# Windows of the projections in another column order, with heads, Fourier products and turns between them

## The reference

```python
for l in range(2):                                  # first_block
    mod = silu_c @ w_ada[l] + b_ada[l]              # 1024 -> 6*1024: shifts, scales and gates
    mc = silu_cc @ w_ada[l][:, :n_c] + ...          # the same for the context tokens
    hx = rmsnorm(x) * (1 + sc_a) + sh_a             # hc likewise from ctx
    ux = hx @ w_in[l]                               # 1024 -> 2304 columns
    uc = hc @ (w_in[l] if l == 0 else w_in[l][:, OFF_K:OFF_HQ])
    fx = fourier_mix(ux[0:256], w_four[l])          # FFT over tokens and channels, then a product
    ax = attention(rope(rmsnorm(q)), rope(rmsnorm(k)), v)   # 8 query heads, 2 key heads of 64
    rx = hgrn_scan(...)                             # gated recurrence in chunks
    x = x + g_a * (concat(fx, ax, rx) @ w_out[l])
    x = x + g_f * swiglu(rmsnorm(x) * (1 + sc_f) + sh_f, w_gate[l], w_up[l], w_down[l])
    # the context likewise in layer 0
for i in range(2):                                  # second_block
    mod = silu(c_2) @ ada_w[i] + ada_b[i]
    h = rmsnorm(x) * (1 + sc1) + sh1
    x = x + g1 * banded_or_dilated_attention(h @ w_in) @ w_out   # 1536 or 2304 columns
    x = x + g2 * swiglu(...)
return rmsnorm(x) * final_norm
```

## Time and profile before

| | us |
|---|---|
| three runs, median (lowest to highest) | 2167.18 (2163.68 to 2167.72) |
| profiled execution | 2165.82 |
| its span in the trace | 2163.9 |
| its mean granted clock of TensorE | 0.896 |

### The profile page before, as it was taken

How to read it: one execution, slowest core, us unless ns; L and a number is a source line. 1 busy time by engine, 2 the same in 40 slices (tenths; PEclk the granted TensorE clock), 3 DMA queues, 4 the chain that set the end, 5 groups by cost and what they waited for, 6 DMA issues and landing times.

```text
span 2163.9 us, 30885 instructions
## 1 busy us (share of the span) xinstructions
PE 1828.9 (85%) x12238; PEld 1639.6 (76%) x12238; DVE 1353.1 (63%) x2508; ACT 834.7 (39%) x1600; POOL 59.9 (3%) x133
## 2 busy tenths in 40 slices
PE   4697688889999998894778699967789989588997
PEld 2696576788887887792567699866689979478996
DVE  1667868456776556527775578856658874565544
ACT  3422453233221321522642344345534435454442
POOL 0000012000000000000020000000000000000000
PEclk8899778789999999896778799987899999699999
DMA  8544010026555553333212688642279865004653
GB/s 283 177 152 136 1 59 21 1 79 175 157 184 156 165 161 129 118 105 98 78 40 78 182 253 273 228 130 54 78 228 273 268 223 152 24 18 121 188 172 136
DMA packets 358990, 300.60 MB, mean 139 GB/s; under 512 B 7920, under 2 KB 333280, under 8 KB 358464
## 3 DMA queue, kind: packets, MB, share of 16 engines
q1 hardware_dynamic: 357456, 294.22, 44.7%
q0 software_dynamic: 1392, 4.42, 0.9%
HBM read 297.56 MB, written 1.05 MB: 138 GB/s over the span
## 4 chain that ended last, share of the span: by engine, by line
PE 72%; DVE 14%; ACT 5%; issue 5%; DMA 4%; SPq 0%; DVEq 0%; ACTq 0%; POOLq 0%
PE bank L793 69%; PE bank L807 3%; ACT whigh L1271 1%; DMA A<-in_w_ada 1%; DVE ACC L1688 1%; ACT PB L1424 1%; DVE A L1769 1%; DMA raw<-in_ffn_w_in 1%; DVE A L1953 1%; DVE HTL L1775 1%; DMA raw<-in_w_up 0%; DMA X<-in_ctx 0%; DVE nw L1707 0%; DVE rs L1709 0%; DVE nw L1708 0%
## 5 line engine op out<-in xcount | busy, mean ns | idle before, releaser
L1672 DVE TENSOR_TENSOR wlow<-raw,whigh 128x2048 fp32r<-128x2048 f32 (+1 forms) x183 | 410.0, 2244 | 328.7 <-ACT whigh L1271 328.0
L1271 ACT ACTIVATE whigh<-raw 128x2048 fp32r<-128x2048 f32 (+1 forms) x183 | 343.2, 1878 | 585.1 <-PE bank L793 362.4
L793 PE MATMUL bank<-HTH,whigh 128*128 128x256 f32 (+1 forms) x1424 | 447.7, 314 | 12.5 <-DVE HTL L1775 12.5
L793 PE MATMUL bank<-HTL,whigh 128*128 128x256 f32 (+1 forms) x1424 | 443.1, 311 | 0.0
L793 PE MATMUL bank<-HTH,wlow 128*128 128x256 f32 (+1 forms) x1424 | 442.8, 311 | 0.0
L793 PE MATMUL bank<-whigh,HTH 128*128 128x256 f32 (+1 forms) x1008 | 292.2, 290 | 12.7 <-DVE HTL L1775 6.0
L793 PEld LDWEIGHTS bank<-HTH,whigh 128*128 128x128 f32 x1424 | 277.1, 195 | 26.0 <-issue 13.6
L1688 DVE SCALAR_TENSOR_TENSOR ACC<-A,cond,ACC 128x256 f32<-128x256 f32 x602 | 282.9, 485 | 17.5
L793 PE MATMUL bank<-wlow,HTH 128*128 128x256 f32 (+1 forms) x1008 | 290.3, 288 | 0.0
L793 PE MATMUL bank<-whigh,HTL 128*128 128x256 f32 (+1 forms) x1008 | 290.0, 288 | 0.0
L793 PEld LDWEIGHTS bank<-HTH,wlow 128*128 128x128 f32 x1424 | 276.5, 194 | 13.2
(11 more groups left out here) (214 smaller groups left out, 2278.9 us busy)
## 6 DMA issues: line engine op xcount, KB each, us to landing
...
```

The source lines that it names most:

```text
L793: return nc.tensor.matmul(out, lhsT, rhs, start=start, stop=stop, skip_group_check=True)
L1271: nc.scalar.activation(parts(loads[n])[0], raw_slot(loads[n]), ACT.Copy).then_inc(*made("split_high", loads[n]))
L1672: V.tensor_tensor(low, raw_slot(loads[n]), as_float(high), ALU.subtract).then_inc(*made("split_low", loads[n]))
```

## The change

It does these things:

- `win_order` gives the windows another order: 0, 3, 1, 2, 4 to 8 in layers 0 and 1 (window 3 holds keys and values), keys and values first in layers 2 (4, 5, 0 to 3) and 3 (6, 7, 8, 0 to 5). `load_plan` and `proj_jobs` follow it.
- In layers 0 and 1 the Fourier products stand after the second tile of the second window, the gains with it, and DVE makes tile t's heads in the window at position t + 3; PE turns the tile after the second tile of the window at position t + 5 (`turns_after`). In layers 2 and 3 the keys are turned one window after the keys' last one, and the queries one window behind their own.
- The heads are now computed in place in `U` and not through a buffer of `A`; `values_low` is a function of its own.
- The chunk sums: two chunks in each of the first four windows of layer 0 instead of one in each of eight; the four chunks in layer 0's heads and the four in layer 1's heads (computed by PE) go; 35 instead of 27 stand beside the feed forward of layer 0. The slots of the first eight lie now in `U`'s columns 1280 to 2304 (`AWU`), two instead of three, and each load is two DMAs of 512 KB.
- The first chunk loads of a feed forward wait for PE's product `h` of the last tile (at the feed forward's start) instead of `g`. `gate_rows` of layer 0's feed forward is moved from `gu` 0 to `gu` 9.
- The load of `w_four` on POOL waits for the turned keys of the layer's last tile.
- Buffers change places to make room: the conditioning bias goes to `U`'s tile 2, the query halves and turned probabilities of layer 3 are swapped in `A`, copies of the keys for the dilated groups are made tile by tile.

The diff, cut to its core:

```diff
+def win_order(layer):
+
+    return ((0, 3, 1, 2, 4, 5, 6, 7, 8), (0, 3, 1, 2, 4, 5, 6, 7, 8), (4, 5, 0, 1, 2, 3), (6, 7, 8, 0, 1, 2, 3, 4, 5))[layer]
...
-    return [(j, t) for j, (a, b) in enumerate(col_groups(layer)) for t in tiles_of(layer, "mix") if cols_of(layer, t, a, b)]
+    groups = col_groups(layer)
+    return [(j, t) for j in win_order(layer) for t in tiles_of(layer, "mix") if cols_of(layer, t, *groups[j])]
...
+def turns_after(layer, j, n):
+
+
+    at = win_order(layer).index(j)
+    if layer < 2:
+        return [("tile", at - 5)] if n == 1 and at >= 5 else []
+    last_k = win_order(layer).index((DH * (HEADS_Q[layer] + HEADS_K[layer]) - 1) // 256)
+    first_q = win_order(layer).index(0)
+    out = [("keys", n)] if at == last_k + 1 else []
+    if n == 1 and at > first_q:
+        out.append(("queries", j - 1))
+    return out
...
+GATES_AT = 9
...
-    give([("win", 0, j) for j in range(8)] + [(0, "heads", t) for t in range(4)] + scan(0, 4))
-    give(feed_forward(0, 27))
-    give([(1, "heads", t) for t in range(4)] + scan(1, 6))
+    give([("win", 0, j) for j in win_order(0)[0:4] for _ in range(2)] + scan(0, 4))
+    give(feed_forward(0, 35))
+    give(scan(1, 6))
...
+        AWU = [U[:, t:t + 2, 1280:2304].rearrange("p t (k c) -> p t k c", k=4) for t in (2, 0)]
...
-            slots = {"start": (0, 1, 2, 3), "projection": (2, 3, 4), "feed_forward": (2, 3, 4)}.get(group[0], (0, 1))
+            slots = {"start": (0, 1, 2, 3), "projection": (5, 6), "feed_forward": (2, 3, 4)}.get(group[0], (0, 1))
...
-                    sp.wait_ge(*upto("product", "mod", 0, STARTING - 1))
+                    sp.wait_ge(*(upto("product", "bias") if slot == 5 else upto("sums_set")))
                 elif group[0] == "feed_forward":
 
-                    sp.wait_ge(*upto("product", "g", group[1], "ffn", 1 if group[1] == 0 else 0, 1))
+                    sp.wait_ge(*upto("product", "h", group[1], "ffn", tiles_of(group[1], "ffn")[-1], 1))
                 w, b = ada_w(l)
-                sp.dma_start(dst, w.rearrange("(p k) c -> p k c", k=8)[:, :, 256 * j:256 * j + 256]) \
-                    .then_inc(*made(f"ada_weights{slot}", l, j, by=16))
+                src = w.rearrange("(p k) c -> p k c", k=8)[:, :, 256 * j:256 * j + 256]
+                if slot < 5:
+                    sp.dma_start(dst, src).then_inc(*made(f"ada_weights{slot}", l, j, by=16))
+                else:
+                    for half in range(2):
+                        sp.dma_start(dst[:, half], src[:, 4 * half:4 * half + 4]).then_inc(*made(f"ada_weights{slot}", l, j, by=16))
...
-                    pool.dma_start(W4, io["w_four"][l].rearrange("(k p) c -> p k c", p=P)).then_inc(*made("gains_in", l, by=16))
...
+                    pool.wait_ge(*upto("product", "kT", l, tiles_of(l, "mix")[-1], 0))
+                    pool.dma_start(W4, io["w_four"][l].rearrange("(k p) c -> p k c", p=P)).then_inc(*made("four_in", l, by=16))
...
             def project(l):
-                for j, (a, b) in enumerate(col_groups(l)):
+                for at, j in enumerate(win_order(l)):
                     key = ("win", l, j)
                     need_parts(key)
                     wh, wl = (w.rearrange("p (k c) -> p k c", k=KD) for w in parts(key))
-                    for t in [t for j2, t in proj_jobs(l) if j2 == j]:
-                        if j == 0 or (l == 1 and t >= 2):
+                    for n, t in enumerate([t for j2, t in proj_jobs(l) if j2 == j]):
+                        if at == 0 or (l == 1 and t >= 2):
                             h_ready(l, "mix", t)
                         ps = open_bank("u", l, j, t)
                         r = slice(P * t, P * t + P)
                         for k in range(KD):
                             last = mm3(ps[:, 0:256], (HTH[:, k, r], HTL[:, k, r]), (wh[:, k, :], wl[:, k, :]), k == 0, k == KD - 1)
                         last.then_inc(*made("product", "u", l, j, t))
+                        if l < 2 and at == 1 and n == 1:
+                            for g in range(2 if l == 0 else 1):
+                                fourier(l, g)
+                        for turns in turns_after(l, j, n):
+                            head_turns(l, *turns)
                     late(key)
                 late(None)
+                modulation_end()
+                if l >= 2:
+                    head_turns(l, "queries", DH * HEADS_Q[l] // 256 - 1)
...
+                        if (l, f) == (0, GATES_AT):
+                            gate_rows(l, "ffn")
...
             def project(l):
-                for j in range(len(col_groups(l))):
+                for at, j in enumerate(win_order(l)):
                     split(index[("win", l, j)] + HIGH)
-                    beside("win", l, j)
+                    if l < 2:
+                        if at == 1:
+                            for g in range(2 if l == 0 else 1):
+                                fourier(l, g)
+                        if at == 2:
+                            gains(l)
+                        beside("win", l, j)
+                        if 5 <= at < 8:
+                            heads_low(l, "tile", at - 5)
+                        if 3 <= at < 7:
+                            heads(l, at - 3)
+                    else:
+                        for turns in turns_after(l, j, 0) + turns_after(l, j, 1):
+                            heads_low(l, *turns)
+                        if j == (DH * (HEADS_Q[l] + HEADS_K[l]) - 1) // 256:
+                            for t in X_TILES:
+                                heads(l, t)
+                    if j == value_group(l):
+                        values_low(l)
+                if l < 2:
+                    heads_low(l, "tile", 3)
+                else:
+                    heads_low(l, "queries", DH * HEADS_Q[l] // 256 - 1)
...
-                need_u(l, tiles[-1], PROJ[l] - 256, PROJ[l]) if l != 1 else need_u(l, tiles[-1], OFF_I, OFF_HQ)
-                need_u(l, 1, PROJ[l] - 256, PROJ[l])
-                for n, t in enumerate(tiles):
-                    if n:
-                        lows(tiles[n - 1])
...
+                if t:
+                    dve.wait_ge(*upto("product", "kT", l, t - 1, 0))
...
@@ -2173,11 +2262,6 @@
                 if l:
                     split(index[last_down(l - 1)] + HIGH)
                 project(l)
-                if l < 2:
-                    gains(l)
-                    for g in range(2 if l == 0 else 1):
-                        fourier(l, g)
-                heads(l)
                 attention(l)
                 if l < 2:
                     recurrence(l)```

What this does to the engines' lists at the places where the time is set. SyncE at the start of layer 0's projection, before (L629 loads projection weights, L592 a chunk's weights; each waits for the product or the sum that frees its buffer):

```order
L629 DMA raw<-in_w_in 128x8x256 [waits product]
L592 DMA A_53<-in_w_ada 128x8x256 [waits product] x3
L592 DMA A_53<-in_w_ada 128x8x256 [waits ada_sum]
L629 DMA raw<-in_w_in 128x8x256 [waits product]
L592 DMA A_53<-in_w_ada 128x8x256 [waits ada_sum]
L629 DMA raw<-in_w_in 128x8x256 [waits product]
```

269 lines of the change are left out of this document (146 added, 123 removed).

## The result

The changed kernel takes 2111.8 us (median of four runs, 2109.38 to 2114.55) against 2167.45 us (2163.68 to 2168.07): a ratio of 0.9747, with a 95% interval of 0.973 to 0.9764. The profiled execution took 2112.47 us, its span is 2110.2. The forecast was 2101, its range 2086 to 2124. So 55.6 us were won where 66.4 were forecast.

A forecast was written before the change was run, and what follows sets the result against it. The prediction took TensorE, with 72% of the chain of waits, to bound the kernel. Its terms, −27 + 1.5 + 9.4 − 31 − 8.5 − 7.8 − 2 − 1, sum to −66.4, giving 2101 us, range 2086 to 2124.

The forecast's parts named there:

- Layer 0's projection: Layer 0, projection to attention: attention starts at about 215 against 242.06, −27, with +1.5 for the clock.
- The pauses: Layer 0's projection: TensorE waits for chunk sums, Fourier gains and tile 0's heads, 17.4 us in all.
- The term for the clock: Layer 0's projection: gaps let the clock fall, one such loss more than now, +1.5 us.
- both sums: Layer 0's second window: VectorE ends the first two chunk sums at 94.1 and 101.2, then split and Fourier copies by 104.9.
- The landing: Layer 0's projection: chunk 8's load arrives so that its sum begins at 87, against 89.69 before.
- Layer 0's feed forward: Layer 0's feed forward: eight more chunks cost 5.6 us of TensorE and a 3.8 us wait, +9.4 in sum.
- Later keys have one each: Layer 0's feed forward: only the key after the first has two chunks, waiting 3.8 us; later keys have one.
- Layer 1's projection: Layer 1, projection to attention: 43.6 us go and 13 come back as heads' wait, turns and tail, −31.
- The feed forwards' starts: Start of layers 1 and 2's feed forwards: earlier chunk loads remove TensorE's wait and low clock, −8.5 and −7.8.
- The first rival: Feed forwards' start: chunk loads and first weights want the same queues, the 16 us stay, 2117; chance 0.16.
- The second rival: Layer 0's chain of load, sum, slot is longer, three later pairs cost 3 us more each, 2112; chance 0.12.
- The third: Layer 0's projection: TensorE stays at the lower clock after repeated pauses, 72 us more, 2173; chance 0.05.

The follow-up runs named there:

- e10_combined0: Changed kernel without chunk sums in layer 0's projection (12 in its scan), VectorE's copies before the split, 31 chunks beside layer 0's feed forward, ten in layer 1's scan: 2060.61 us.
- e1_dve_order: Changed kernel, but in layers 0 and 1 VectorE does Fourier copies and chunk sums of the second and third window before the weights' split: 2100.49 us.
- e7_early_window_loads: Changed kernel, but SyncE issues the first two window chunks' loads before waiting for the end of the first window: 2113.28 us.
- e2_single_ffn0: Changed kernel, but 32 chunks in place of 35 beside layer 0's feed forward, one per key, and nine in place of six in layer 1's scan: 2102.88 us.
- e6_last_key_free: Changed kernel, but 31 chunks beside layer 0's feed forward, one per key, none on the last, and ten in layer 1's scan: 2103.79 us.
- e4_before_early: Kernel before, with only the feed forwards' first chunk loads waiting for `h` in place of `g`: 2158.63 us.
- e8_combined: Changed kernel, VectorE's copies, sums and heads before the split in three windows, 31 chunks beside layer 0's feed forward, ten in layer 1's scan: 2088.26 us.

## Why the prediction was right, and where it was off

- **Layer 0's projection, −25.5 forecast, −25.3 measured.** The total is right by luck, since two of its terms are not. The pauses were put at 17.4 us in five places and were 12.2 in three: 5.29 for 6.8, 5.00 for 4.5 and 1.92 for 2.1; those of 0.8 and 3.2 didn't come. The term for the clock was +1.5, for one more dip. There were three behind these pauses: 0.50 from 103 to 108 costs 2.5 us, 0.77 from 108 to 113 1.2, 0.50 from 139 to 144 2.5, 0.72 from 164 to 170 1.7, some 8 together, where the dip of before cost 2.4 (from 96.78, where TensorE starts again, 0.6 up to 98 and then 1.8). That is 5.5 more. The dip in the first window, from 70.29 to 76.15, costs 2.9 more, behind a pause that both kernels have. So the pauses were overstated by 5 and the clock understated by 4 to 7; with all of this some 2 us are left that went the other way and weren't followed. The step that failed is "one such loss more than now", taken from a single row; the low level after a pause of 5.29 us lasted some 7 us here (all of 103 to 108, 2.3 of the next five), after one of 10.16 us in the kernel before some 5 (from 96.78, then 3.6 of the six from 98), not the 3 that the prediction read. `e10_combined0` shows what the pauses cost with the clock: without them 28.7 us less, of which 7 are the chunk products.
- **What made the first pause.** The prediction had both sums end at 101.2 and let the copies follow. In truth the sums ended at 97.9 and the copies waited for a split that ScalarE could not start before the window's last copy. `e1_dve_order` and `e7_early_window_loads` show this from both sides.
- **The landing.** I kept 87 against the rule of the Trainium skill, "DMA: Bandwidth & Descriptors", section "🔬 Queues, rings and completion order", by which it would be near 84. It was 83.89, 7.7 us after the issue at 76.21: the rule, not my reading of the 14.1 us, fits this trace. Why it took 14.1 us in the kernel before stays open. The landing moved no time, as `e7_early_window_loads` shows.
- **Layer 0's feed forward, +9.4 forecast, +20.2 measured.** This is the step that carried the error of the whole. "Later keys have one each" was wrong: 35 chunks on 32 keys make three pairs, and the last key has a chunk as well. The two further pairs cost 1.67 and 2.12 us of waiting for `modc` (the second chunk's product waits until ScalarE has taken the first's), and 1.7 for the clock; the last key's sum 3.0 in the norm; the first pair 3.61 for 3.8, with 1.7 of low clock behind it. With the 5.6 of the chunk products these make 19.5 of the 20.2. `e2_single_ffn0` and `e6_last_key_free` take 13.3 and 3.4 of it away. It could have been counted from the plan. Spreading the window chunks over more windows in place of pairing them wasn't tried: their slots lie in columns of `U` that the later windows write.
- **Layer 0's scan, 0 forecast, +5.2 measured.** Whether it is the change's isn't shown. For a difference by chance: `e4_before_early` has the lists of the kernel before up to there and took 183.0 us, that kernel 178.7. Against it: all five profiles with the changed kernel's own projection took 183.8 to 184.5, and the two in which VectorE's order in the projection was changed (`e1_dve_order`, `e8_combined`) 177.7 and 175.6, with the same lists in this stretch. The low clock comes at other places of the scan there: the ten us from the 70th behind the start of attention are at 1.00 in the changed kernel and at 0.68 in `e1_dve_order`. What decides it is open, and so a part of what those two won may be owed to their projection.
- **Layer 1's projection, −31 forecast, −35.1 measured.** The mechanism was right. The one wait for heads of 2.7 is 2.65 in two places (1.11 and 1.54), the tail 5.61 for 5 to 5.5. The surplus is in the rows of before: the stretch with Fourier products and heads ran at a low clock, the last eight products took 3.75 us where they take 1.98 in the changed kernel, and the forecast moved them at their old length. This explains 1.8 of the 4; the rest wasn't followed further.
- **The feed forwards' starts, −8.5 and −7.8 forecast, −8.9 and −7.0 measured**, and shown from both sides. The first rival is refuted.
- **The second rival** (later pairs of loads too slow) is refuted: in the projection no sum waits for a DMA after the first. **The third** (clock stays low) came about in part: 0.91 on the mean from 71 to 209, where the projection before had 0.96. The rule of the Trainium skill, "TensorE: Matmul & The Clock Gate", section "HAM oscillation — how this bites in real kernels", that repeated pauses throttle again, agrees with the trace: three pauses, three stretches at 0.50 to 0.72, where `e10_combined0`, without them, has 1.00 from 76 to 182. It was worth some 8 us, 5.5 more than before, not 72.
